# Token-major mixer output and down projections, and a moved order in the group stage, in a one-core encoder layer

## The reference

```
h = rmsnorm(x, mix_pre);  proj = h @ w_in            # 2048 -> 17,000 columns
y_ssm = ssd_mixer(...) @ w_ssm_out                   # 8 groups, conv, scan, gated norm
y_attn = dsa_mixer(...) @ w_attn_out                 # 16 heads
merged = sigmoid(gA) * y_ssm + sigmoid(gB) * y_attn
x = x + rmsnorm(merged @ w_mix_out, norm_mix_post)   # M: 2048 x 2048
h = rmsnorm(x, norm_ffn_pre)
u = causal_dwconv(h @ w_up, width 3)                 # U: 2048 x 8192
x = x + rmsnorm((gelu(u1) * u2) @ w_down, norm_ffn_post)  # D: 4096 x 2048
rmsnorm(x, g) = x * rsqrt(mean(x * x over features) + 1e-6) * g
```

## Time and profile before

| | before |
|---|---|
| median of 3 runs | 1956.62 us |
| the profiled execution | 1960.62 us, span 1958.9 us |
| PE busy | 1861.7 us, 95% |
| DVE busy, ACT busy | 1346.9 us, 1137.8 us |
| POOL busy | 116.2 us |
| chain that ended last | PE 85%, DVE 5%, ACT 4% |
| DMA | 340.72 MB, mean 174 GB/s |

### The profile page before, as it was taken

The page is one execution under the profiler, slowest core; times in us unless marked ns, Lnnn a source line. Parts: engine busy times, 40 slices in busy tenths (PEclk is TensorE's granted clock), DMA queues, the critical chain, the costliest instruction groups (busy, mean ns, idle before and its releaser), DMA issues.

```text
span 1958.9 us, 37740 instructions
## 1 busy us (share of the span) xinstructions
PE 1861.7 (95%) x10552; PEld 1589.4 (81%) x10552; DVE 1346.9 (69%) x2595; ACT 1137.8 (58%) x2265; POOL 116.2 (6%) x186
## 2 busy tenths in 40 slices
PE   6999999999999999999999999995699999999997
PEld 5878878778778878888888888784588888888885
DVE  4656677787777787777755656556777777775555
ACT  5445566666666666667655555454566666664443
POOL 0000000000010010111100000012000000000000
PEclk9999999999999999999999999998899999999998
DMA  6646556655665665566655555653366666656552
GB/s 168 195 142 186 177 161 183 191 158 177 182 181 151 182 182 152 171 180 182 185 190 186 189 180 188 200 186 105 97 185 190 182 185 190 182 175 192 187 185 97
DMA packets 427371, 340.72 MB, mean 174 GB/s; under 512 B 28864, under 2 KB 422704, under 8 KB 426816
## 3 DMA queue, kind: packets, MB, share of 16 engines
q1 hardware_dynamic: 422368, 325.14, 55.3%
q0 software_dynamic: 3904, 14.75, 2.4%
q10 hardware_dynamic: 1056, 0.32, 0.1%
HBM read 337.96 MB, written 2.16 MB: 174 GB/s over the span
## 4 chain that ended last, share of the span: by engine, by line
PE 85%; DVE 5%; ACT 4%; issue 4%; ACTq 1%; DVEq 1%; POOL 0%; POOLq 0%
PE bank L1294 54%; PE bank L1296 27%; PE bank L1301 3%; ACT w_hi L468 2%; DVE cc L962 1%; ACT cc L557 1%; PE bank L1536 1%; DVE w_lo L794 1%; DVE mo L1178 0%; DVE x_t L1185 0%; PE bank L1407 0%; ACT tmp L475 0%; DVE yn L1079 0%; ACTq L454 0%; DVE o_s L951 0%
## 5 line engine op out<-in xcount | busy, mean ns | idle before, releaser
L794 DVE TENSOR_TENSOR w_lo<-raw,w_hi 128x512 fp32r<-128x512 f32 x1224 | 851.6, 703 | 488.0 <-ACT w_hi L468 477.5
L468 ACT ACTIVATE w_hi<-raw 128x512 fp32r<-128x512 f32 x1224 | 757.6, 629 | 471.5 <-PE bank L1296 462.6
L1294 PE MATMUL bank<-h_s,w_hi 128*128 128x512 f32 x2592 | 937.3, 405 | 6.5 <-DVE h_s L1127 4.0
L1296 PE MATMUL bank<-h_s,w_lo 128*128 128x256 f32 x2592 | 729.0, 281 | 0.0
L1294 PEld LDWEIGHTS bank<-h_s,w_hi 128*128 128x128 f32 x2592 | 489.3, 189 | 133.5 <-issue 14.0
L1296 PEld LDWEIGHTS bank<-h_s,w_lo 128*128 128x128 f32 x2592 | 491.6, 190 | 0.6
L1294 PE MATMUL bank<-o_s,w_hi 128*128 128x512 f32 x1280 | 456.3, 401 | 10.4 <-DVE w_lo L794 5.6
L1294 PE MATMUL bank<-y_s,w_hi 128*128 128x512 f32 x1024 | 362.4, 399 | 1.4 <-DVE w_lo L794 1.4
L1296 PE MATMUL bank<-o_s,w_lo 128*128 128x256 f32 x1280 | 361.0, 282 | 0.0
L1294 PEld LDWEIGHTS bank<-o_s,w_hi 128*128 128x128 f32 x1280 | 242.3, 189 | 72.0 <-DVE w_lo L794 5.9
L1296 PE MATMUL bank<-y_s,w_lo 128*128 128x256 f32 x1024 | 287.6, 281 | 0.0
(11 more groups left out here) (182 smaller groups left out, 1025.9 us busy)
## 6 DMA issues: line engine op xcount, KB each, us to landing
raw<-in_w_in SPq DMA_DIRECT2D x576, 256.0 KB, 2.9
raw<-in_w_up SPq DMA_DIRECT2D x256, 256.0 KB, 3.2
raw<-in_w_ssm_out SPq DMA_DIRECT2D x128, 256.0 KB, 2.9
raw<-in_w_down SPq DMA_DIRECT2D x128, 256.0 KB, 3.0
raw<-in_w_attn_out SPq DMA_DIRECT2D x64, 256.0 KB, 3.0
raw<-in_w_mix_out SPq DMA_DIRECT2D x64, 256.0 KB, 3.1
cs_rows<-cs_dram POOLq DMA_DIRECT2D x16, 512.0 KB, 5.5
cs_rows<-cs_dram POOLq DMA_DIRECT2D x16, 256.0 KB, 6.2
```

The source lines that it names most:

```text
L468: act.activation(w_hi[:, c % 4, :, :], raw[:, slot, 2 * m:2 * m + 2, :], ACT.Copy).then_inc(hi_done, 1)
L794: dve.tensor_tensor(w_lo[:, c % 4, :, :], raw[:, (c // 2) % 4, 2 * (c % 2):2 * (c % 2) + 2, :], w_hi[:, c % 4, :, :].bitcast(F32), ALU.sub ...
L1294: pe.matmul(bank[b][:], w_hi[:, w[0], w[1], w[2]], src[:, k0 + k, :], start=start and k == 0, stop=False, skip_group_check=True)
L1296: last = pe.matmul(bank[b][:, T:2 * T], w_lo[:, w[0], w[1], w[2]], src[:, k0 + k, 0:T], start=False, stop=True, skip_group_check=True)
```

## The change

1. **Group stage.** The decays and `weights_of_head` stand two halves higher up the list; the second mask one half higher; the second head's attention, the `c_b` product and the first transposes of `xc` one half lower.
2. **M and D are token-major.** A wide half has one 128-row tile of the contraction and 512 output columns. PE takes the activation tile (128 features x 128 tokens) as the stationary operand and moves 512 weight columns: for each of two token blocks, rounded x `w_hi`, rounded x `w_lo`, rest x `w_hi`. The two banks of a run hold the finished sums of 128 tokens by 512 features each. SP loads 512 columns in a row (`wide`).
3. **Norms along the row.** ScalarE squares the bank and sums it along the row in the same instruction (`wide_sq`), VectorE multiplies the bank by a gain that a DMA has spread over the partitions (`wide_gain`), and the reciprocal of the root is one value per token (`inverse`). POOL's sums, the ones-matmuls, the transposes of x in M's loop and those ahead of the output are gone.
4. **Into U.** x2 is token-major. PE transposes it against a diagonal of the reciprocals (`h2_bank`), four tiles ahead of U and the other twelve between its first halves; ScalarE and VectorE split each tile out of the bank.
5. **Around it.** Two of ScalarE's fourteen parameter loads go; a dummy root ahead of M's and of D's loop (`load_root`) brings ScalarE's table.

```diff
 # ScalarE, group stage
-                    if j == 13:
+                    if j == 14:
                         attention_exp(i, 1)
...
-                    if 22 <= j < 38 and j % 2 == 0:
-                        decays(i, (j - 22) // 2)
+                    if 20 <= j < 36 and j % 2 == 0:
+                        decays(i, (j - 20) // 2)
 # VectorE, group stage
-                    if j in (15, 25):
-                        mask_rows(i, j // 25)
-                    if j == 22:
+                    if j in (15, 24):
+                        mask_rows(i, j // 24)
+                    if j == 23:
                         x_dt(i, 0)
 # PE, group stage
-                        if j == 11:
+                        if j == 12:
                             logits(i, 1)
...
-                        if j == 21:
+                        if j == 22:
                             x_tok(i, 0)
 # PE, M and D
+            def wide_half(i, per, c, src, kt, b):
+                pe.wait_ge(lo_done, i * per + (c + 1))
+                hi = w_hi[:, c % 4, :, :].rearrange("p k c -> p (k c)")
+                low = w_lo[:, c % 4, :, :].rearrange("p k c -> p (k c)")
+                for t in range(2):
+                    for w, at in ((hi, 0), (low, 0), (hi, T)):
+                        last = pe.matmul(bank[b + t][:], src[:, kt, at + P * t:at + P * t + P], w,
+                                         start=kt == 0 and w is hi and at == 0, stop=True, skip_group_check=True)
+                last.then_inc(half_used, 1)
...
+            def h2_bank(kt):
+                if kt >= 4:
+                    pe.wait_ge(h2_split, kt - 3)
+                for t in range(2):
+                    last = mm(bank[4 + kt % 4][:, P * t:P * t + P], x2[:, t, P * kt:P * kt + P], diag2[:, t, :])
+                last.then_inc(h2_mm, 1)
 # ScalarE
+            def wide_sq(i, per, h, n, k, use, junk):
+                act.wait_ge(half_used, i * per + (h + 1))
+                for t in range(2):
+                    q = i * 4 + (2 * k + t)
+                    act.wait_ge(main_out, i * 4 + (n + 2 * k + t))
+                    dst = stat[:, use, q:q + 1] if isinstance(q, int) else stat[:, use, bass.ds(q, 1)]
+                    act.activation(junk[:], bank[2 * k + t][:], ACT.Square, accum_out=dst).then_inc(main_out, 1)
...
+            def load_root():
+                act.activation(eps[:, 4:6], eps[:, 2:4], ACT.Sqrt)
...
+            for n in range(8):
+                t, q = n // 4, n % 4
+                act.wait_ge(x2_done, n + 1)
+                if n:
+                    act.wait_ge(x2_sq, n)
+                act.activation(mix_junk[:], x2[:, t, WIDE * q:WIDE * q + WIDE], ACT.Square,
+                               accum_out=stat[:, 1, 2 * q + t:2 * q + t + 1]).then_inc(x2_sq, 1)
 # VectorE
+            for n in range(8):
+                t, q = n // 4, n % 4
+                at = slice(WIDE * q, WIDE * q + WIDE)
+                dve.scalar_tensor_tensor(out=x2[:, t, at], in0=gained[:, t, at], scalar=stat[:, 0, 12 + t:13 + t],
+                                         in1=x_again[:, t, at], op0=ALU.mult, op1=ALU.add).then_inc(x2_done, 1)
+            inverse(1, lambda: dve.wait_ge(x2_sq, 8))
+            for t in range(2):
+                dve.tensor_scalar(diag2[:, t, :], ident[:], stat[:, 1, 12 + t:13 + t], None, ALU.mult).then_inc(diag2_done, 1)
```

More of the change, by code:

```diff
@@ L85 @@
 MISC_G = MISC_Q + GROUPS * MISC_S
-MISC_M = MISC_G + GROUPS
-PAR_LOADS = 14
+PAR_LOADS = 12
+WIDE = 512
+H2_TURNS = [range(6)] + [(2 * j + 4, 2 * j + 5) for j in range(1, 6)] + [(), ()]
 class Links:
@@ L145, in build @@
         eps, at = place("eps", [P, 8], F32, at)
+        stat, at = place("stat", [P, 3, 16], F32, at)
         mt_b, _ = place("mt_b", [P, 2, 3 * P], F32, at)
@@ L334, in _ @@
             u = HALF["M"] // 2
-            with sp.Fori(0, 8) as i:
-                for m in range(4):
-                    plain(wmix, m, i * 256, i * 4 + (u + m), m)
+            with sp.Fori(0, 4) as i:
+                for m in range(8):
+                    wide(wmix, m, i * WIDE, i * 8 + (u + m), m % 4)
             u = HALF["U"] // 2
@@ L417, in _ @@
                                        ALU.add).then_inc(sq_added, 1)
-            def sum_squares(done, added, turns):
-                link(pool.memset(sq_sum[:], 0.0))
-                linked()
-                with pool.Fori(0, turns) as i:
-                    for n in range(2):
-                        pool.wait_ge(sq_done, i * 2 + (done + n + 1))
-                        pool.wait_ge(sq_added, i * 2 + (added + n))
-                        pool.tensor_tensor(sq_sum[:], sq_sum[:], sq[:, n, :], ALU.add).then_inc(sq_added, 1)
             pool.wait_ge(half_used, HALF["M"])
@@ new lines, in root @@
+            def root(use):
+                act.wait_ge(summed, use + 1)
+                act.activation(stat[:, use, 10:12], stat[:, use, 8:10], ACT.Sqrt, scale=1.0 / D,
+                               bias=eps[:, 0:1]).then_inc(rooted, 1)
+            def load_root():
+                act.activation(eps[:, 4:6], eps[:, 2:4], ACT.Sqrt)
+            load_root()
+            with act.Fori(0, 2) as i:
+                for k in range(2):
+                    for j in range(16):
+                        split(i, 32, H + 16 * k + j + LEAD)
+                    wide_sq(i, 32, H + 16 * k + 15, N, k, 0, mix_junk)
@@ new lines, in inverse @@
+            def inverse(use, squares):
+                squares()
+                dve.tensor_reduce(stat[:, use, 8:10], stat[:, use, 0:8].rearrange("p (n t) -> p t n", t=2), AXIS.X,
+                                  ALU.add).then_inc(summed, 1)
+                dve.wait_ge(rooted, use + 1)
+                dve.reciprocal(stat[:, use, 12:14], stat[:, use, 10:12]).then_inc(inverted, 1)
+                dve.wait_ge(inverted, use + 1)
+            with dve.Fori(0, 2) as i:
+                for k in range(2):
+                    for j in range(16):
+                        lo(i, 32, H + 16 * k + j + LEAD)
+                    if k == 0:
+                        dve.wait_ge(gain_in[0], 16)
+                    wide_gain(i, 4, N + 2 * k, 2 * k, mix_gain, k)
@@ L1510, in _ @@
-            pe.wait_ge(sq_added, 56)
-            total(MISC_M + 1)
-            H, N = HALF["U"], TILE["U"]
-            with pe.Fori(0, 16) as i:
+                        if first and k == 0:
+                            pe.wait_ge(h2_split, 2 * j + 2)
+                        half(i, 16, H + 8 * k + j, o_s, 2 * j, 2 * k, 2 * k + 1, j == 0)
+                        if first and k == 0 and j < 6:
+                            for kt in (2 * j + 4, 2 * j + 5):
+                                h2_bank(kt)
@@ L1516, in _ @@
+            up_turn(0, True)
+            with pe.Fori(1, 16) as i:
+                up_turn(i, False)
+            H, N = HALF["D"], TILE["D"]
+            with pe.Fori(0, 2) as i:
                 for k in range(2):
                     pe.wait_ge(tile_out, i * 4 + (N + 2 * k - 2))
-                    for j in range(8):
-                        pe.wait_ge(h2_split, 2 * j + 2)
-                        half(i, 16, H + 8 * k + j, o_s, 2 * j, 2 * k, 2 * k + 1, j == 0)
-            H, N = HALF["D"], TILE["D"]
```

297 lines of the change are left out of this document (110 added, 187 removed).

## The result

The changed kernel takes 1878.8 us (median of 4 runs, 1872.15 to 1888.07) against 1956.67 us (4 runs beside it): ratio 0.9606, 95% interval 0.9555 to 0.9658. The forecast was 1899.0 with a range of 1884 to 1915. The profiled run took 1872.15 us.

What follows compares the result with a forecast made beforehand. TensorE, busy 1861.7 of 1958.9 us, was taken as the bound, leaving matmul work or holes between matmuls. Terms -20, 0, -23.8, -3.6, -10.7, +1.5 and -1.0 summed to -57.6: median 1956.62 to 1899.0 us, range 1884 to 1915.

Steps and rivals of the forecast that it cites:

- the group stage: Stage from 226 to 798 us: reordered blocks remove TensorE's waits for `mt` and `o_s`; -20 us, bounds -24.8 and -10.
- the wide halves: M and D: six 512-column matmuls replace four of 512 and four of 256; no change, ends -6 and +5 us.
- M to U: From M's last matmul to U's eighth half: 53.9 us becomes 30.1, saving 23.8, ends 27 and 14.
- 0.6 us of new wait: Group stage, half 30: TensorE arrives earlier for the second `xc` transposes and waits for the silu; 0.6 us per group.
- the small slips around each wait: Group stage: small delays around the removed waits go too, taking the saving from 19 to 20 us.
- The even share: M and D: the 0.034 us a pair takes beyond its columns falls equally on each matmul; 192 halves save 6 us.
- the rule quoted: Trainium skill: weight loads overlap matmuls only for other row groups; fewer bare loads would save 41 us. The prediction rejected it.
- U to D: Ahead of D's loop: the dummy root's table load on ScalarE is unhidden while TensorE waits; +1.5 us, or 0.
- The group stage gives its gain back: Rival, group stage: moved blocks land on halves that already have one; gain 5 instead of 20, total 1914 us; chance 0.12.
- the hand-overs cost more: Rival, M to U and end: U's first turn stays at half clock, output writes bind; total 1913 us; chance 0.08.
- The loads come out: Rival, M and D: stationary loads no longer hide under matmuls; 219 us over 192 halves, total 2118; chance 0.03.
- Wide halves are cheaper: Rival, M and D: wide halves cost less, by the equal split of a pair's overhead; total 1893 us; chance 0.12.

Runs made afterwards that it cites:

- the second profile of the kernel after: Profile from running the changed kernel once more with no edit; the median of those 5 runs was 1877.63 us, ratio 0.96.

## Why the prediction was wrong

Two terms were too small: the group stage by 9.8 us, and the wide halves, put at nothing, by 5 to 10. The group stage (-29.8), M to U (-20.9), the end (-11.2), the transposes of x (taken at -3.6), G (-1.5), the start (-1.2), D's load (+1.5) and the wide halves at -5.1 to -10.6 add up to -71.8 to -77.3 us, where the forecast had -57.6.

**Group stage (-20; measured -29.8).** The mechanism was right: all waits named went, the one left is at the first `xc` transposes (1.1 us in all; 0.1 a group was foretold), and the two moves do what was said of each. Two sizes were off. "0.6 us of new wait" in half 30 did not come: 4.8 us over the groups. The step said VectorE would stand behind its taps "as before, or only a little earlier", while the order already showed mask and weights ahead of them; the taps began 3.7 us earlier, PE asked 4.3 us earlier, and 0.4 us of slack was left. And "the small slips around each wait", taken as 1, were 6.1. Of these 2.5 come from the rows, which count idle time from a recorded end that lies behind the next possible start; 2.6 from two stretches at half clock that went with the `mt` waits (the step priced a wait by its idle time and nothing behind it, though the earlier trace rows has the clock at 0.99 there); 0.8 from the logits' own matmuls. So the bound "all 24.8 us saved at best" was no bound.

**Wide halves (0, ends -6 and +5; measured -10 in M and D together).** The value was read from starts rounded to 0.01, 0.24. The even share, 0.230, came nearest of the three, and the pitch is 0.2267. Both were worked out from a pair of 354 ns, which was the slow of two values. The quick pair of 347 ns would have given 13.3 ns a matmul and 1.36 a half, -10.6 by 192 halves against 1.415. M gave 3.3 beyond the transposes and D 6.7 beyond its load. About half of that is luck: against the quick pair (1.387 a half) wide halves save 0.027 a half, 5.1 us in all. The old D took 182.5 us in the trace compared here and 179.3, on the same code, in the profile of the kernel with decays and weights up. That the loads stay hidden, against the rule quoted, was right.

**M to U (-23.8; measured -20.9 by starts, 32.7 us against 30.1).** From M's last end: the products began after 3.2 (forecast 3.1), PE stood still until 11.7 (11.6). From there on it cost more: U began at 15.1 (13.6), because sixteen cold records took 3.4 us, and its first turn took 17.6 (16.5), with 6 x 0.81 for the products in place of 3.4 in all. From profile to profile the stretch itself moves: with 10.2 us at half clock in place of 13.7, the second profile of the kernel after took 31.9 us by starts, not 33.2. The failed term is "a 128-column transpose is 0.12": the row used has one record a tile, and these have two. U's turn was warm from its second half on.

**Transposes of x (-3.6)** are part of M's -6.9 and not measured apart. **The end (-10.7; measured -11.2)**: 12.1 foretold, 11.9 found; products at 0.67 in place of 0.75, landing 2.4 to 3.1 us, so the writes do not bind. **U to D (+1.5)**: the wait is 3.1 us, 2.9 foretold, but in about half of the profiles it cost another 1.6 in clock, which no term held. **The start (-1.0)**: 29.6 became 28.6.

**The profiled execution.** The sum was made against 1960.6 us, which had the slow pair nearly everywhere. The execution profiled afterwards had the quick one: 11.7 us in O and U between these two traces are chance, and no part of the change. G's 1.5 came in every pair of profiles and has no cause shown.

**The rivals.** "The group stage gives its gain back" and "the hand-overs cost more" failed: 29.8 and U's turn warm. "The loads come out" failed. "Wide halves are cheaper" was the true one, at 0.12; its -6 is near the 5.1 against the quick pair and too small for the 10.6 against the slow one. The range ended at 1884 because the lower side held only -6, -5 and -3, two of them exceeded; with -9.8 and -10 it would have reached the measured time.

## What to carry to other kernels

Take the gain of a removed wait from the starts of the two instructions around it, before and at a place without a wait, and not from the idle time alone; then look at the granted clock behind it. Work out a price that is multiplied by a thousand instructions from a long stretch with its count, not from two starts, and do it in two stretches, since the same code can show two values. For an operation that a trace has under several lines, count its records per call before its price is used, and look up which lines of the code issue it the same way.

## What the runs showed of the hardware

- A matmul at full clock took its columns at 2.4 GHz and 13.3 ns: 0.2267 us for 512, 0.120 for 256, with a new 128 x 128 stationary tile for each, the load hidden in both. At half clock 512 columns took 0.427 us, with nothing beside.
- TensorE's waits of 1.70 us in the group stage were followed by 3.4 us at a granted clock of 0.5 in one or two of eight groups; behind the 3 us wait in D that came in five profiles of nine. It cost about 1.5 us each time.
- The alternation of 512 and 256 columns runs at 347 or 353 ns a pair, for hundreds of us at a time, without a difference in the granted clock; four long and then four short ran at one value, 1.402 us a half.
- A product with a float32 diagonal of 128 columns is two records, 0.20 us; the transposes against the identity are one, 0.12.
- ScalarE's table load could not be moved into a loop by moving the one instruction that needs it: a load then stood at the loop's head and another inside.
